# A two-way RWKV-7 scan: two half-height products stacked into one full-height product, and turns in the transposing form

## The reference

```python
def _wkv7_step(S, inp):
    r_t, w_t, k_t, v_t, aa_t, bb_t = inp
    sa = jnp.einsum('zbhij,zbhj->zbhi', S, aa_t)
    S = S * w_t[..., None, :] + sa[..., :, None] * bb_t[..., None, :] + v_t[..., :, None] * k_t[..., None, :]
    y = jnp.einsum('zbhij,zbhj->zbhi', S, r_t)
    return S, y
```

## Time and profile before

| | |
|---|---|
| median of 3 runs | 4858.02 us (4856.51 to 4867.45) |
| profiled execution | 4869.98 us, span 4867.9 us |
| TensorE | busy 4311.4 us (89%), 50,312 matmuls and as many weight loads |
| VectorE | busy 1928.2 us (40%) |
| ScalarE | busy 1292.7 us (27%) |
| GpSimd | busy 1279.7 us (26%) |
| mean granted clock of TensorE | 0.954 |

### The profile page before, as it was taken

The page is one execution under the profiler, slowest core; times in us unless marked ns, Lnnn a source line. Parts: engine busy times, 40 slices in busy tenths (PEclk is TensorE's granted clock), DMA queues, the critical chain, the costliest instruction groups (busy, mean ns, idle before and its releaser), DMA issues. The chain is left out here.

```text
span 4867.9 us, 112762 instructions
## 1 busy us (share of the span) xinstructions
PE 4311.4 (89%) x50312; PEld 3614.9 (74%) x50312; DVE 1928.2 (40%) x3380; ACT 1292.7 (27%) x2542; POOL 1279.7 (26%) x794
## 2 busy tenths in 40 slices
PE   3899898999999996996958888888878999999997
PEld 2688856888888885885847777777755888888886
DVE  3011054154252443226146666666633244242441
ACT  1111065211011112236124444444422211011110
POOL 2111032311111115111125454555512311111110
PEclk8899999999999997998979999999989999999998
DMA  3211242311313112121232222221222311313214
GB/s 130 65 59 55 69 134 73 119 39 53 107 40 105 56 58 80 69 78 43 85 89 67 67 68 72 63 74 56 63 100 87 126 35 50 111 40 100 65 50 161
DMA packets 402639, 372.41 MB, mean 77 GB/s; under 512 B 63057, under 2 KB 370513, under 8 KB 399985
## 3 DMA queue, kind: packets, MB, share of 16 engines
q1 hardware_dynamic: 390320, 354.75, 23.6%
q10 hardware_dynamic: 11840, 10.49, 0.6%
HBM read 257.68 MB, written 107.48 MB: 75 GB/s over the span
## 5 line engine op out<-in xcount | busy, mean ns | idle before, releaser
L422 POOL TENSOR_TENSOR f_wlow<-f_raw,f_whigh 128x1024 fp32r<-128x1024 f32 (+1 forms) x152 | 360.1, 2369 | 1671.2 <-ACT f_whigh L493 1671.2
L478 PE MATMUL f_ps<-fx_hh,f_whigh 128*128 128x512 f32 (+1 forms) x2112 | 529.6, 359 | 0.0
L478 PE MATMUL f_ps<-fx_hl,f_whigh 128*128 128x512 f32 (+1 forms) x2112 | 528.5, 358 | 0.0
L478 PE MATMUL f_ps<-fx_hh,f_wlow 128*128 128x512 f32 (+1 forms) x2112 | 528.2, 358 | 0.0
L493 ACT ACTIVATE f_whigh<-f_raw 128x1024 fp32r<-128x1024 f32 (+1 forms) x152 | 156.6, 1030 | 922.7 <-PE f_ps L478 895.0
L478 PEld LDWEIGHTS f_ps<-fx_hl,f_whigh 128*128 128x128 f32 x2112 | 348.7, 189 | 65.8
L478 PEld LDWEIGHTS f_ps<-fx_hh,f_whigh 128*128 128x128 f32 x2112 | 348.5, 189 | 65.6
L478 PEld LDWEIGHTS f_ps<-fx_hh,f_wlow 128*128 128x128 f32 x2112 | 348.2, 188 | 65.7
L478 PE MATMUL f_ps<-mo_oh,f_whigh 128*128 128x512 f32 (+1 forms) x1440 | 360.8, 359 | 26.2 <-POOL f_wlow L422 26.2
L1605 PE MATMUL sc_inv_ps<-sc_tf,sc_bl 64*64 64x64 f32 x6400 | 283.0, 223 | 105.3 <-DVE sc_tf L1956 59.8
L478 PE MATMUL f_ps<-mo_ol,f_whigh 128*128 128x512 f32 (+1 forms) x1440 | 360.4, 359 | 0.0
(11 more groups left out here) (268 smaller groups left out, 8383.8 us busy)
## 6 DMA issues: line engine op xcount, KB each, us to landing
f_xo<-xres SPq DMA_DIRECT2D x64, 640.0 KB, 4.0
xres<-f_xo SPq DMA_DIRECT2D x56, 640.0 KB, 2.9
f_raw<-in_ffn_w_gate SPq DMA_DIRECT2D x44, 512.0 KB
f_raw<-in_ffn_w_up SPq DMA_DIRECT2D x44, 512.0 KB
sc_rk<-rkvl SPq DMA_DIRECT2D x80, 256.0 KB, 3.4
rkvl<-ri_ot SPq DMA_DIRECT2D x28, 640.0 KB, 2.9
f_raw<-in_ffn_w_down SPq DMA_DIRECT2D x32, 448.0 KB
qkv_raw<-in_na_w_qkv SPq DMA_DIRECT2D x24, 512.0 KB, 5.7
```

Source lines behind the costliest of these rows:

```text
L422: nc.gpsimd.tensor_tensor(wlow[:, m % 2, 0:kt], raw[:, 0:kt], whigh[:, m % 2, 0:kt].bitcast(F32), ALU.subtract).then_inc(cut_lo, 1)
L478: last = nc.tensor.matmul(ps[:, m % 2, n, 0:count], w[:, m % 2, k], x[:, k, t0:t0 + count], start=(k == 0 and w is whigh and x is xh), sto ...
```

## The change

Tokens of b' or U (rows 0 to 63) and of k~ or v (rows 64 to 127) are stacked on the 128 rows, so that a sum of two products of height 64 becomes one product of height 128. Each head and direction gets a slot of its own along the free dimension.

- Gram: one matmul of 64 rows by 128 columns for b' and k~ together, for two.
- Turns: `nc.tensor.transpose` of b' and k~ together (64x128), and of v with the 64 columns ahead of it in `vpad`, so that v comes out on rows 64 to 127.
- X: one product with `gx[..., 0]` (a above ga) and `sv[:, ., 0]` (S above v). ScalarE copies a to `gx` (`query_copy`), in two instructions of 64 rows x 512.
- State: the copy of S by the identity, both heads in one matmul of 128 columns, then one product with `t0` (b' above k~) and `sv[:, ., 1]` (U above v). All its output lies on rows 0 to 63, as does that of U.
- y: one product with r of S, then one with `gx[..., 1]` (both parts of nr) and `sv[:, ., 1]`. For the second head r is copied to rows 0 to 63 by ScalarE (`read_copy`, 64 x 512).
- `bm` is copied out of the Gram's PSUM by ScalarE (`bm_copy`, two of 64 rows x 256 a direction) without its mask; VectorE's `gram_out` waits for it and has two products (64 x 512 and 128 x 512) for three. The level masks of the inverse are as before.
- Turn copies: v is copied twice (64 x 512 each) beside one copy of b' and k~ (128 x 512).
- y has two buffers for three, and two stores a group for three.

```diff
@@ gram
-                    for s in range(U):
-                        u = unit(z, s)
-                        for a in range(2):
-                            for rows in halves:
-                                last = nc.tensor.matmul(gram_ps[rows, a, s * 128:(s + 1) * 128], rec[rows, r, z, u, a],
-                                                        rec[rows, r, z, u, 2:4].rearrange("p a n -> p (a n)"), start=True, stop=True)
+                    for u in range(U):
+                        for h, rows in enumerate(halves):
+                            last = nc.tensor.matmul(gram_ps[:, slot(h, z), u * 128:(u + 1) * 128], rec[rows, r, z, u, 0:2].rearrange("p a n -> p (a n)"),
+                                                    rec[rows, r, z, u, 2:4].rearrange("p a n -> p (a n)"), start=True, stop=True)
...
@@ turn
-                        for a in range(2):
-                            for rows in halves:
-                                nc.tensor.matmul(turn_ps[z][rows, 0, a * W + s * C:a * W + (s + 1) * C], rec[rows, r, z, u, a], ident[rows, rows],
-                                                 start=True, stop=True)
-                        for rows in halves:
-                            last = nc.tensor.matmul(turn_ps[z][rows, 1, s * C:(s + 1) * C], vb[rows, r, z, u * C:(u + 1) * C], ident[rows, rows],
-                                                    start=True, stop=True)
+                        for h, rows in enumerate(halves):
+                            nc.tensor.transpose(turn_ps[z][:, slot(h, z), u * C:(u + 1) * C], rec[rows, r, z, u, 0:2].rearrange("p a n -> p (a n)"),
+                                          ident[rows, rows])
+                        for h, rows in enumerate(halves):
+                            at = z * W + u * C
+                            last = nc.tensor.transpose(turn_ps[z][:, slot(h, z), W + u * C:W + (u + 1) * C], vpad[rows, r, at:at + 2 * C], ident[rows, rows])
...
@@ x_product
+                        pe.wait_ge(a_al, G + 1)
...
+                        for h in range(2):
+                            last = nc.tensor.matmul(x_ps[side(h, z), z], gx[:, G % 4, z, slot(h, z), u, 0], sv[:, G % 2, 0, z, u, slot(h, z)],
+                                                    start=True, stop=True)
@@ u_product
-                            last = nc.tensor.matmul(u_ps[rows, z], rf[side(h, z), G % 3, z, s], xs[side(h, z), z], start=True, stop=True)
+                            q = slot(h, z)
+                            last = nc.tensor.matmul(u_ps[:, q, z * C:(z + 1) * C], rf[halves[q], G % 3, z, unit(z, s)], xs[halves[q], z],
+                                                    start=True, stop=True)
@@ s_product
+                        nc.tensor.matmul(s_ps[:, z], ident[0:HD, 0:HD], sv[0:HD, G % 2, 0, z, unit(z, s)].rearrange("p q n -> p (q n)"),
+                                         start=True, stop=False)
+                    for q in range(2):
+                        for z in range(Z):
+                            u = unit(z, s)
+                            last = nc.tensor.matmul(s_ps[:, z, q * C:(q + 1) * C], t0[:, G % 2, z, q, u], sv[:, G % 2, 1, z, u, q],
+                                                    start=False, stop=q == 1)
@@ y_products
+                    pe.wait_ge(a_rl, G + 1)
...
+                                r = rl[0:HD, z, u] if h else rec[0:HD, G % 4, z, u, 3]
+                                nc.tensor.matmul(y_ps[rows, z, to], sv[0:HD, G % 2, 0, z, u, slot(h, z)], r, start=True, stop=False)
+                        for z in range(Z):
+                            for h, rows in enumerate(halves):
+                                q = slot(h, z)
+                                last = nc.tensor.matmul(y_ps[rows, z, to], sv[:, G % 2, 1, z, u, q], gx[:, G % 4, z, q, u, 1], start=False, stop=True)
@@ ScalarE
+                def bm_copy(G, z):
+                    act.wait_ge(pe_gram[z], G + 1)
+                    if G >= 1:
+                        act.wait_ge(g_bl[z], G)
+                    for h, rows in enumerate(halves):
+                        src = strided(gram_ps[0:HD, slot(h, z)], 0, [[2 * C, U], [1, C]])
+                        last = nc.scalar.activation(bm[rows, z], src, ACT.Copy)
+                    last.then_inc(a_bm[z], 1)
...
+                        if s < 2 and group(I + 2):
+                            bm_copy(I + 2, s)
+                        if s == 0 and group(I + 1):
+                            query_copy(I + 1)
...
+                        if s == 3 and group(I):
+                            read_copy(I)
                         p_copy(I + 1, 3 * s + 2)
@@ VectorE, gram_out
-                    dve.wait_ge(pe_gram[z], G + 1)
...
+                    dve.wait_ge(a_bm[z], G + 1)
...
+                    nc.vector.tensor_tensor(to[HD:P, :, 0], gram[HD:P, :, 0:C], strict, ALU.mult)
+                    nc.vector.tensor_tensor(to[:, :, 1], gram[:, :, C:2 * C], incl, ALU.mult).then_inc(d_gram[z], 1)
```

More of the change, by code:

```diff
@@ L1440, in rwkv_scan @@
         t_ps = [b[:, 256:512] for b in inv_ps]
-        x_ps, u_ps, s_ps = (chain_ps[:, :, i * C:(i + 1) * C] for i in range(3))
+        x_ps, u_ps, s_ps = chain_ps[:, :, 0:C], chain_ps[0:HD, :, C:3 * C], chain_ps[0:HD, :, 4 * C:6 * C]
         y_ps = low_ps[:, :, 0:W]
@@ L1530, in _ @@
                 store_y(NG - 1)
-                for s in range(3):
-                    sp.wait_ge(y_stored[s], 48 * len(range(s, NG, 3)))
+                for s in range(2):
+                    sp.wait_ge(y_stored[s], 32 * len(range(s, NG, 2)))
                 for s in range(2):
@@ L1649, in x_product @@
                             pe.wait_ge(d_gram[z], G + 1)
+                        pe.wait_ge(a_al, G + 1)
                     for z in range(Z):
-                        for h, rows in enumerate(halves):
-                            nc.tensor.matmul(x_ps[side(h, z), z], ga[rows, G % 3, z, s], vt[rows, G % 2, z, s], start=True, stop=False)
-                    for z in range(Z):
-                        for h, rows in enumerate(halves):
-                            last = nc.tensor.matmul(x_ps[side(h, z), z], rec[rows, G % 4, z, unit(z, s), 2], st[rows, (4 * G + s) % (2 * U), z],
-                                                    start=False, stop=True)
+                        u = unit(z, s)
+                        for h in range(2):
+                            last = nc.tensor.matmul(x_ps[side(h, z), z], gx[:, G % 4, z, slot(h, z), u, 0], sv[:, G % 2, 0, z, u, slot(h, z)],
+                                                    start=True, stop=True)
                     last.then_inc(pe_x, 1)
@@ L1881, in queries @@
                     nc.vector.tensor_tensor(rec[:, r, :, :, 2], uc(kk[:, G % 2]), ex0_of, ALU.mult)
[L1882 to L1883 removed]
+                    for h, rows in enumerate(halves):
+                        kept = strided(keep[rows], j * U, [[NC + (NS - 1 - 2 * j) * U, Z], [1, U]])
+                        ends = strided(exb[rows], C, [[U * (C + 1) - C, Z], [C + 1, U]])
+                        last = nc.vector.tensor_tensor(strided(pc[0:HD, r], h, [[2 * U + 1 - 2 * h, Z], [2, U]]), ends, kept, ALU.mult)
+                    last.then_inc(d_rec, 1)
                 def bonus_out(G):
```

124 lines of the change are left out of this document (58 added, 66 removed).

## The result

The stacked kernel takes 4937.17 us (median of 4 runs, 4928.09 to 4943.01), the kernel before beside it on the same chip 4860.77 us (4 runs): a ratio of 1.0154, with a 95% interval from 1.0132 to 1.0177. It is slower by 76 us where 11 us less were forecast, and it lies above the range of 4800 to 4905 us. The profiled execution took 4941.97 us, with a span of 4940.0.

A forecast was written before the change was run, and what follows sets the result against it. Scan rounds were taken as bound by the later of TensorE's stream or VectorE/ScalarE copies, plus instruction-supply stalls: 24.8 + 1.75 + 0.05 = 26.55 us against 26.83, -11 us over 38 rounds, giving 4847 us; range 4800 to 4905.

The forecast's parts named there:

- The sum of the segments: One scan round, cut at starts of inverse blocks: 24.8 us without instruction-supply stalls, +1.75 us for the change, 26.55 with 0.05 of stalls.
- INV(9) to INV(1): Scan round between starts of inverse blocks 9 and 1: 5.90 us, forecast +0.25 from the state product and VectorE's copies.
- INV(1) to INV(3): Scan round between starts of inverse blocks 1 and 3: 4.89 us, let go by VectorE, forecast +0.3.
- INV(3) to INV(6): Scan round between starts of inverse blocks 3 and 6: 6.93 us, TensorE-filled up to block 5, forecast +1.2, y alone +1.0.
- INV(6) to INV(7): Scan round between starts of inverse blocks 6 and 7: 3.02 us, set by VectorE's two running sums and copy, forecast unchanged.
- INV(7) to INV(9): Scan round between starts of inverse blocks 7 and 9: 4.28 us including 0.25 of stall; state +0.4, turn -0.4, net 0.
- The stops: TensorE idle in the scan for lack of instructions ("issue"): 2.0 us a round before, 0.05 allowed after.
- The costs of the changed products: TensorE time of changed scan blocks: state 0.64 to 0.95 us, Gram 1.64 to 0.86, turn 0.80, y 2.74.
- The changes of form: Switches of TensorE tiling form in the scan: 4 a round before, about 31 after, 0.10 us each.
- The longer blocks are not paid back: Rival, chance 0.27: y's form changes and those around state add 2.7 us, stalls worth 1.5; round 28.0 us, 4903 us.
- Supply is all that matters: Rival, chance 0.20: only instruction supply counts and the longer blocks hide; round 25.6 us, 4812 us.
- The clock falls: Rival, chance 0.08: TensorE does less, one scan round in five runs at 1.2 GHz; +91 us, 4940 us.

## Why the prediction was wrong, step by step

**The sum of the segments was right, in part by luck.** 26.55 us a round were forecast, and a clean round has 26.43. By segment, from the medians of the 17 clean rounds: INV(9) to INV(1) 6.35 (forecast 6.15), INV(1) to INV(3) 5.41 (5.2), INV(3) to INV(6) 8.24 (8.1), INV(6) to INV(7) 2.36 (3.02), INV(7) to INV(9) 4.07 (4.03). Three segments are longer than forecast by 0.55 us together, and INV(6) to INV(7) is shorter by 0.66. That is VectorE: both running sums last 0.66 us now, and one had lasted 1.18 in the round that I took for before, though only 18 of the 74 running sums of its 37 rounds last over 0.75 us, and TensorE waits for VectorE ahead of INV(7) in only 7 of these rounds. Ahead of INV(3) the order of events is the forecast one, and ScalarE's two copies (0.76 us for 0.66) and VectorE's two products (1.32 for 1.18) are the 0.2 us more.

**The stops** were priced at 2.0 us a round by a subtraction, 26.83 less 24.8, and the added blocks at 1.75. A clean round of before takes 26.65 on average and one of after 26.56, so the two cancel as forecast. Each by itself wasn't measured. What speaks for the price is that the clean rounds of before spread from 25.04 to 28.07 us, the shortest near the 24.8 taken for a round without stops, while those of after take 26.4 to 26.5 us or 26.95 and nothing else. The weight loads' "issue" of all kinds in the 37 rounds fell from 151 to 94 us.

**The costs of the changed products** stand in the clean round above. y runs from 2618.88 to its last row, which begins at 2621.54 and holds eight starts: 2.89 us from the first start to the last (forecast 2.74). The Gram takes 0.89 (forecast 0.86) and the state 0.99 (0.95). One more term was too high: a turn is 0.49 us from its first row to its last, not 0.80. Its 16 matmuls start 0.06 us apart on each of two tiles, where I had taken 0.107, the spacing of 128 columns; the profile shows their moving operand with 64 columns.

**The changes of form** were taken at 0.10 us each. On the trace of weight loads they show as "issue" of 0.17 us ahead of each state block and 0.33 ahead of the first X:
```profile
2610.55 0.54 PEld L1676 LDWEIGHTS sc_chain_ps<-sc_sv,sc_t 128*64 128x64 f32 x8 [0.17 <-issue]
```
```profile
L1603 PEld LDWEIGHTS sc_inv_ps<-sc_tf,sc_bl 64*64 64x64 f32 x6400 | 242.7, 145 | 196.8 <-ACT sc_pt L1781 90.2 <-issue 56.0 <-ACT sc_pt_last L1781 31.7
L1676 PEld LDWEIGHTS sc_chain_ps<-sc_sv,sc_t 128*64 128x64 f32 x1280 | 95.7, 150 | 31.3 <-issue 31.3
```
This also spoils one of my signs: "issue" at the inverse's loads was to fall to a tenth and is 56.0 us for 52.0. It is not the same thing any more. In a clean round the same nine gaps between loads that start over 0.25 us apart come back to the hundredth. Two stand ahead of INV(1) and INV(7), where the matmul waits for VectorE; the other seven, 1.26 us in all, stand at a change of form. Before, they came at ever other places and were up to 1.8 us long. The Trainium skill (TensorEngine Tiling, Key Properties) has the drain at a change of form; the trace agrees at seven of about 31 changes, with 0.12 to 0.33 us each. So as causes of the loss the rivals "The longer blocks are not paid back" and "Supply is all that matters" both fall: at full clock the round is what the sum says.

**The step that failed is the clock.** The forecast times all 38 rounds at 2.4 GHz and gives "The clock falls" a chance of 0.08. Half of the rounds were hit. That rival's time, 4940 us, is what came, but by other parts: it had one round in five at +12 us, and the trace has 13 of 37 at +4.6 and six at +1.4, with 12 us more at the end of the scan: that the sums agree is luck. The rival even named the place ("a 1.6 us gap ahead of INV(3)"). The sum booked the longer wait there as +0.3 us on the path, and put what it does to the clock at nothing; in the 37 rounds the low clock took 70 us, for 6 before. With a wait of 1.05 us of standing still there were two falls in 37 rounds. At 1.58 there are nineteen in that place, at 1.62 in the kernel before sixteen. With the wait filled (1.14 or 0.27 us of standing still left), or with INV(3) at X's heels, there is none. Where the wait was moved, in the run with all of y ahead of INV(3), the falls moved with it. The same 1.58 us had only three to seven falls in that place in the three runs with a longer round.

**What stays open.** Why the same wait brings the clock down in some rounds and not in others, and why a fall lasts 13.7 us in the stacked kernel and 3.4 in the kernel before with the long wait; the blocks behind it are not the same (one Gram block of 16 matmuls and 2.9 us of y for 32 and 1.9), but no run separates them. Whether the length of the round decides how many rounds are hit, and whether the transposing form has a part. And the last rounds: with the falls gone from the middle (four and twelve matmuls in the wait) the rounds are 0.2 us shorter than before's, yet the whole is 0.2 to 0.3% slower; 6 to 7 us of that is the scan's end (73 to 74 us for 66.8, with 23 to 27 us at 1.2 GHz for 10), which no run took apart. The profiles can't settle such small sums: that of the kernel before is of an execution 12 us above its median, and outside the scan the profiled executions differ by several us (3731 us before, 3723 with twelve matmuls).

## What to carry to other kernels

A wait on TensorE can cost more than its length, when the clock falls behind it: look at the granted clock by stretch, find what stands ahead of the first fall, and remove or fill that wait first. Fill it with useful work that fits: y whole was too long and opened the next hole and y by halves gave 0.9964. A layout that trades instructions for longer blocks should be judged after its new waits have been ordered away; as changed here it lost 1.5%, and with its copies in another order it gained 0.5%. The same order gave the old layout nothing, so an order has to be judged anew in each kernel: there VectorE's running sums came to lie beside GpSimd's products and lasted up to 1.7 us for 0.66.

## What the runs showed of the hardware

A wait of 1.6 us was enough to bring the clock down in 16 to 19 of 37 rounds, in kernels whose TensorE is at work for 85% of a round (22.50 of 26.40 us in the stacked one). A fall of 13.7 us costs 4.6 us, one of 3.4 us 1.4. The transposing form is one pair of a weight load and a matmul for fp32 operands of 64x128, and 16 of them on two tiles take 0.72 us with the last one's length, where the plain form adds 1.2 us a round. Four small matmuls a round (1.4% of its pairs) in that wait took 68 us off the scan's rounds, with 1.14 us of it still empty. And a running sum of 128x256 on VectorE takes 0.65 to 0.69 us alone and up to 1.7 with GpSimd's products beside it.
